# A grouped mixture of experts with its gate, up and down passes in loops of their own

## What is computed

```python
x = layer_norm(ALPHA * x + (1 + g1) * y, ln_mix_g[l], ln_mix_b[l])
h = x * (1 + sc2) + sh2
y = grouped_moe(h, router_w, router_b, w_gate[l], w_up[l], w_down[l])
x = layer_norm(ALPHA * x + (1 + g2) * y, ln_ffn_g[l], ln_ffn_b[l])
...
def expert_block(args):
    xb, e = args
    return (jax.nn.silu(xb @ w_gate[e]) * (xb @ w_up[e])) @ w_down[e]
```

## Time and profile before

| what | us |
| --- | --- |
| median of 3 runs | 1334.7 |
| lowest, highest | 1334.52, 1337.36 |
| the profiled execution as timed | 1341.6 |
| its span, first to last instruction | 1339.5 |
| TensorE busy in it | 1090.9 |
| VectorE busy | 429.8 |
| ScalarE busy | 175.0 |

### The profile page before, as it was taken

How to read it: one execution, slowest core, us unless ns; L and a number is a source line. 1 busy time by engine, 2 the same in 40 slices (tenths; PEclk the granted TensorE clock), 3 DMA queues, 4 the chain that set the end, 5 groups by cost and what they waited for, 6 DMA issues and landing times.

```text
span 1339.5 us, 31050 instructions
## 1 busy us (share of the span) xinstructions
PE 1090.9 (81%) x13118; PEld 644.4 (48%) x13118; DVE 429.8 (32%) x1378; ACT 175.0 (13%) x423; POOL 21.1 (2%) x61
## 2 busy tenths in 40 slices
PE   5999988658998579657899989696599996796675
PEld 1885445224554235323475864363266562463332
DVE  0598152112332113212453431521133331131124
ACT  1104130001010001001201430310011110000011
POOL 1300000000000000000000000000000000000000
PEclk8899989889999889988999999598899998898788
DMA  9975599999999999999996533799999899999990
GB/s 354 383 311 208 224 426 423 425 425 423 424 425 425 425 426 424 424 423 424 416 422 274 239 126 121 321 416 423 425 427 423 342 407 424 425 424 423 424 413 36
DMA packets 56959, 494.74 MB, mean 369 GB/s; under 512 B 4196, under 2 KB 12420, under 8 KB 17176
## 3 DMA queue, kind: packets, MB, share of 16 engines
q1 hardware_dynamic: 55920, 490.75, 88.3%
q10 hardware_dynamic: 744, 2.35, 0.5%
q0 software_dynamic: 192, 0.15, 0.0%
HBM read 492.19 MB, written 1.05 MB: 368 GB/s over the span
## 4 chain that ended last, share of the span: by engine, by line
PE 52%; DMA 41%; DVE 4%; ACT 2%; issue 1%; SPq 0%; DVEq 0%; ACTq 0%; POOLq 0%
PE PS L1122 22%; DMA ring<-in_w_up_dram 17%; DMA ring<-in_w_gate_dram 13%; PE PS L1021 6%; PE PS L1280 4%; DMA ring<-in_w_down_dram 3%; DMA ring<-in_w_kvf_dram 3%; PE PS L1150 2%; DMA work<-in_w_gate_dram 2%; PE PS L1101 2%; PE PS L920 2%; PE PS L1038 2%; DMA ring<-in_w_ada_dram 2%; PE PS L1407 2%; PE PS L1113 1%
## 5 line engine op out<-in xcount | busy, mean ns | idle before, releaser
L1122 PE MATMUL PS<-ring,work 128*32 128x256 f32 x8160 | 518.0, 409 | 171.4 <-DMA ring<-in_w_gate_dram 64.4
L1122 PEld LDWEIGHTS PS<-ring,work 128*32 128x32 f32 x8160 | 280.5, 116 | 391.0 <-issue 116.5
L1728 DVE TENSOR_TENSOR work<-work,PS 128x256 f32<-128x256 f32 x43 | 18.1, 421 | 406.1 <-PE PS L1122 406.1
L1021 PE MATMUL PS<-ring,work 128*128 128x512 f32 x192 | 83.4, 594 | 0.5 <-ACT work L854 0.5
L698 ACT ACTIVATE work<-PS 128x256 f32<-128x256 f32 x43 | 16.5, 384 | 406.0 <-PE PS L1122 406.0
L920 PE MATMUL PS<-ring,cact 128*32 128x512 f32 x384 | 50.7, 668 | 16.1 <-DMA ring<-in_w_ada_dram 16.1
L1101 PE MATMUL PS<-hs,work 128*32 128x256 f32 x784 | 57.7, 414 | 3.8 <-DVE work L1689 3.8
L1280 PE MATMUL PS<-work,ring 128*128 128x256 f32 x256 | 59.0, 394 | 1.4 <-ACT work L630 1.4
L1122 PE MATMUL PS<-work 128*32 128x256 f32 x864 | 52.0, 380 | 9.4 <-DMA work<-in_w_gate_dram 5.4
L1150 PE MATMUL PS<-work 32*128 32x256 f32 x784 | 56.1, 400 | 3.8 <-DVE work L1741 3.8
L1021 PEld LDWEIGHTS PS<-ring,work 128*128 128x128 f32 x192 | 36.2, 190 | 46.5 <-issue 45.7
(11 more groups left out here) (259 smaller groups left out, 871.4 us busy)
## 6 DMA issues: line engine op xcount, KB each, us to landing
ring<-in_w_gate_dram SPq DMA_DIRECT2D x58, 2048.0 KB, 34.3
ring<-in_w_up_dram SPq DMA_DIRECT2D x58, 2048.0 KB, 34.6
ring<-in_w_down_dram SPq DMA_DIRECT2D x58, 2048.0 KB, 28.4
ring<-in_w_ada_dram SPq DMA_DIRECT2D x24, 2048.0 KB, 21.1
work<-in_w_up_dram SPq DMA_DIRECT2D x6, 2048.0 KB, 20.8
work<-in_w_gate_dram SPq DMA_DIRECT2D x6, 2048.0 KB, 33.8
work<-in_w_down_dram SPq DMA_DIRECT2D x6, 2048.0 KB, 42.2
ring<-in_w_pw_dram SPq DMA_DIRECT2D x8, 1024.0 KB, 12.1
```

Source lines behind the costliest of these rows:

```text
L1021: last = pe.matmul(PS[:, banks + 2 * t + q, :], moving[:, k, t * P:(t + 1) * P], quarter(index + h, kk, KH)[:, q * BANK:(q + 1) * BANK], s ...
L1122: last = pe.matmul(dst[SLOTS * s:SLOTS * (s + 1), :], rows[:, cc, SLOTS * q:SLOTS * (q + 1)], quarter(load + h, kk, KH)[:, QUART * s:QUART ...
```

## The change

Four things are changed.

1. All experts but the **first** now run the three loops `gated`, `raised` and `result_of`; only expert 0 keeps `hidden_of`. 
2. In `gated` the next block's token sum stands **ahead** of the gate strips and its transpose between the two strips. VectorE applies the scale into a scratch tile `XM`, waits for `gate_done`, and adds the shift into `XT` (`take_xT_late`).
3. In `raised` VectorE, and no longer ScalarE, copies the kept tokens to `XU`, as the first thing of each block. `XU` is a tile of its own.
4. The final norm is two operations for each token tile: (sum - mean) x gain, then x rstd + offset. ScalarE copies the gain from PSUM to SBUF beforehand (`last_gain`, in `hs`).

ScalarE further waits with its copy to `XT_all` until TensorE has read the residual, which lies in the same memory (`rT_turned`).

```diff
                 def gated(n, j):
                     act.wait_ge(XT_copied, n + l)
+                    act.wait_ge(rT_turned, 2 * l + 2)
                     act.activation(XT_all[:, bass.ds(j * QUART, QUART)], XT.rearrange("p c s -> p (c s)"), ACT.Copy).then_inc(XT_kept, 1)
+                    take_x(n + 1)
                     act.wait_ge(gate_done, n)
                     act.activation(hhT_all[:, bass.ds(j * QUART, QUART)], gate_ps, ACT.Silu).then_inc(sil_ready, 1)
-                    take_x(n + 1)
-
-                def raised(last, j, every):
-                    act.wait_ge(up_done, last)
-                    act.wait_ge(X_turned, every + (l + 1))
-                    act.activation(Xg, XT_all[:, bass.ds(j * QUART, QUART)], ACT.Copy).then_inc(XU_ready, 1)
-                    act.wait_ge(hh_turned, last + 1)
+
+                def raised(n, j):
+                    act.wait_ge(hh_turned, n)
...
             moe(1)
+            act.wait_ge(spread, GAIN_SPREAD)
+            act.activation(last_gain, PS[:, 6:8, :].rearrange("p b n -> p (b n)"), ACT.Copy).then_inc(gain_kept, 1)
...
                     pe.wait_ge(XT_copied, last + (l + 1))
                     pe.wait_ge(hhT_kept, before_all + 1)
                     pe.wait_ge(sil_ready, last)
+                    sum_x(last + 2)
                     strips(load, 0, XT, gate_ps, gate_half)
+                    turn_x(last + 2)
                     strips(load, 1, XT, gate_ps, gate_done)
-                    sum_x(last + 2)
-                    turn_x(last + 2)
...
-                    if e < E - 1:
+                    if e == 0:
                         with pe.Fori(0, blocks):
                             hidden_of(pe.snap(n_pe) + 1, index + 6 * e)
...
+                def take_xT_late(n, kept):
+                    dve.wait_ge(X_turned, n + (l + 1))
...
+                    dve.tensor_tensor(split(XM), split(XT_ps), over[0], ALU.mult).then_inc(XT_begun, 1)
+                    dve.wait_ge(XT_begun, n + (l + 1))
+                    dve.wait_ge(XT_kept, kept)
+                    dve.wait_ge(gate_done, n)
+                    dve.tensor_tensor(XT.rearrange("p c (q s) -> p c q s", q=STRIPS), split(XM), over[1], ALU.add).then_inc(XT_copied, 1)
+
                 def raised(n, j):
+                    dve.tensor_copy(XU, XT_all[:, bass.ds(j * QUART, QUART)]).then_inc(XU_ready, 1)
+                    dve.wait_ge(sil_ready, n)
                     dve.wait_ge(up_done, n)
...
                             next_block(dve.snap(n_dve) + 1)
-                            dve.wait_ge(XT_kept, dve.snap(k_dve) + 1)
-                            take_xT(dve.snap(n_dve) + 2)
+                            take_xT_late(dve.snap(n_dve) + 1, dve.snap(k_dve) + 1)
...
                 for t in range(TT):
+                    link(dve.scalar_tensor_tensor(out=xs[:, t, :].rearrange("p (b n) -> p b n", b=STRIPS),
+                                                  in0=PS[:, 0:STRIPS, QUART * t:QUART * (t + 1)], scalar=mv[:, t, 0:1],
+                                                  in1=last_gain.rearrange("p (b n) -> p b n", b=STRIPS),
+                                                  op0=ALU.subtract, op1=ALU.mult))
+                    dve.scalar_tensor_tensor(out=xs[:, t, :], in0=xs[:, t, :], scalar=rstd[:, t:t + 1], in1=offset,
+                                             op0=ALU.mult, op1=ALU.add).then_inc(done, 1)
```

More of the change, by code:

```diff
@@ L208, in trunk_kernel @@
         r_before = part(E * E, to="p (e f) -> p e f", e=E)
+        XU = r_before.rearrange("p e f -> p (e f)")
         r_hit = part(TT * E, to="p (t e) -> p t e", t=TT)
         r_pos = part(TT * E, to="p (t e) -> p t e", t=TT)
+        XM = work[:, at[0]:at[0] + QUART]
         r_ge = part(2 * GROUPS * PER * PER, to="p (r i j) -> p r i j", i=PER, j=PER)
@@ L276, in trunk_kernel @@
         rT_ready = sem("rT_ready")
+        rT_turned = sem("rT_turned")
         router_in = sem("router_in")
@@ L1076, in residual @@
                                 bank, at = 2 * (k // KH) + half, QUART * t + k % KH
-                                pe.matmul(PS[:, bank, at:at + QUART - 3:KH], rT[of, k, t * P:(t + 1) * P], ident[of, of],
-                                          start=(t == 0 and k % KH == 0), stop=True, tile_position=(64 * half, 0),
-                                          skip_group_check=True)
+                                last = pe.matmul(PS[:, bank, at:at + QUART - 3:KH], rT[of, k, t * P:(t + 1) * P], ident[of, of],
+                                                 start=(t == 0 and k % KH == 0), stop=True, tile_position=(64 * half, 0),
+                                                 skip_group_check=True)
+                                if t == TT - 1 and k == KD - 1:
+                                    last.then_inc(rT_turned, 1)
                 if l == 0:
@@ L1176, in gated @@
                     pe.wait_ge(sil_ready, last)
+                    sum_x(last + 2)
                     strips(load, 0, XT, gate_ps, gate_half)
+                    turn_x(last + 2)
                     strips(load, 1, XT, gate_ps, gate_done)
-                    sum_x(last + 2)
-                    turn_x(last + 2)
                 def raised(n, load, kept, every):
                     pe.wait_ge(XU_ready, kept)
-                    strips(load + 2, 0, XU, up_ps, up_half)
-                    strips(load + 2, 1, XU, up_ps, up_done)
+                    of_kept = XU.rearrange("p (c s) -> p c s", c=NC)
+                    strips(load + 2, 0, of_kept, up_ps, up_half)
+                    strips(load + 2, 1, of_kept, up_ps, up_done)
                     pe.wait_ge(hhT_kept, n)
@@ L1594, in close_sublayer @@
                     return
+                dve.wait_ge(gain_kept, 1)
+                spreads[0] += 1
+                offset = spread_banks(4)
                 for t in range(TT):
-                    last = dve.tensor_scalar(xs[:, t, :].rearrange("p (b n) -> p b n", b=STRIPS),
-                                             PS[:, 0:STRIPS, QUART * t:QUART * (t + 1)], mv[:, t, 0:1], rstd[:, t:t + 1],
-                                             ALU.subtract, ALU.mult)
-                link(last)
-                row = spread_banks(6)
-                for t in range(TT):
-                    last = dve.tensor_tensor(xs[:, t, :], xs[:, t, :], row, ALU.mult)
-                last.then_inc(spread_used, 1)
-                dve.wait_ge(spread_used, spreads[0])
-                with_row(4, lambda t: xs[:, t, :], lambda t: xs[:, t, :], ALU.add, done)
+                    link(dve.scalar_tensor_tensor(out=xs[:, t, :].rearrange("p (b n) -> p b n", b=STRIPS),
[4 more added lines that the diff above has]
+                                             op0=ALU.mult, op1=ALU.add).then_inc(done, 1)
             def ranks(rank, values, rows):
@@ L1718, in next_block @@
                     build_G(n + 1)
+                def take_xT_late(n, kept):
+                    dve.wait_ge(X_turned, n + (l + 1))
+                    split = lambda tile: tile.rearrange("p (c q s) -> p c q s", c=NC, q=STRIPS)
+                    over = [acol[:, (OF_FFN0, OF_FFN1)[l], i, :].rearrange("p (q c) -> p c q", c=NC).unsqueeze(3).to_broadcast([P, NC, STRIPS, SLOTS])
+                            for i in range(2)]
+                    dve.tensor_tensor(split(XM), split(XT_ps), over[0], ALU.mult).then_inc(XT_begun, 1)
[3 more added lines that the diff above has]
+                    dve.tensor_tensor(XT.rearrange("p c (q s) -> p c q s", q=STRIPS), split(XM), over[1], ALU.add).then_inc(XT_copied, 1)
                 def raised(n, j):
+                    dve.tensor_copy(XU, XT_all[:, bass.ds(j * QUART, QUART)]).then_inc(XU_ready, 1)
+                    dve.wait_ge(sil_ready, n)
                     dve.wait_ge(up_done, n)
```

10 lines of the change are left out of this document (6 added, 4 removed).

## The result

The changed kernel takes 1348.3 us (median of 6 runs, 1345.15 to 1352.86) against 1334.6 for the kernel before beside it (6 runs): ratio 1.0102, 95% interval 1.0084 to 1.0121. It is slower by 13.7 us where 6.0 were forecast. The profiled execution took 1346.4 us, its span is 1344.7.

A forecast was written before the change was run, and what follows sets the result against it. Expert stages were taken as DMA-bound, TensorE time counting only where a late load finds the queue empty or behind the last load. +10.7 + 0 - 2.6 - 2.1 = +6.0 gave 1340.7 us; forecast 1337.5 to 1345, range 1331 to 1349.

The forecast's parts named there:

- outer range: Whole kernel: 1331 to 1349 us, taking in no change and most of layer 0's price.
- the lateness in layer 0: Layer 0, blocks 3, 2, 2: -2.7 + 5.9 + 5.9 = 9.1 us late against 11.7 free; cost nought.
- Head wait: Head of each expert: TensorE stands still 2.55 us until VectorE has built the next `G`.
- gate period: Gate loop: 2.00 us wait between blocks plus 4.75 us of work, so one gate block each 6.75 us.
- The up period: Up loop: 1.4 us from up to up with `turn_hh` inside it, so one up pass each 4.85 us.
- The clock rival: Experts 5 and 6: waiting TensorE is granted a lower clock, costing 15 us, time 1356; chance 0.04.
- The stretch: Experts 4, 5, 6 of layer 1: expert 4 ends 2.7 us earlier, expert 6 ends 10.7 us late.
- The 10.1 us to landing: Layer 1, up 0 of expert 8: lands 10.1 us after issue, so cost 10.7 us (8.0 with 7.4 to landing).
- the forecast's own rule: Late loads: lateness costs nothing up to the time to landing less 7.4 us; layer 0 has 11.7 us free.
- Behind the last load: End of kernel: last expert gains 2.6 us (-1.4 gate to up, -1.2 up to up), final norm 2.1.
- Faster: Rival: `G` is ready when asked for, TensorE's stretch gets no longer, DMA hole closes; 1325 us, chance 0.18.
- Slower in both layers: Rival: 0.5 us more on each wait, layer 0 loses 3.9, layer 1 7.5 more; 1352.1 us, chance 0.12.

The follow-up runs named there:

- head_filled: Changed kernel plus 12 matmuls of 128 columns that nobody reads at the head of each expert, ahead of its first token sum: 1.0107 of the kernel before.
- after_again: The changed kernel, unchanged, run and profiled a second time: 1.0096 of the kernel before.
- before_again: The kernel before, unchanged, run and profiled a second time: ratio 0.9992, profiled span 1334.9 us.
- layer0_only: Changed kernel with the new loops of experts 1 to 14 in layer 0 only; last experts and final norm as in the change: 1.0002 of the kernel before.
- last_only_again: Repeat of the changed kernel with the old two loops for all experts but the last: 0.9971 of the kernel before.
- norm_only: Kernel before with only the new final norm (two operations per token tile, ScalarE's copy of the gain): 0.9969 of the kernel before.
- last_only: Changed kernel with the old two loops for all experts but the last, new final norm kept: 0.9959 of the kernel before.
- g_ahead: Changed kernel with VectorE building each block's `G` one block earlier, between the two `XT` operations: 0.9976 of the kernel before.

## Why the prediction was right and wrong

The direction, the mechanism and the place in layer 1 were right, and 1348.3 lies within the outer range of 1331 to 1349, near its end, but over the forecast's own 1337.5 to 1345. The size was not right. The step that failed worst is the lateness in layer 0: it was put at 9.1 us, under the 11.7 that were free, and so its cost at nought, where the lateness was 11.3 to 13.8 and the cost about 3.1. Of the 7.7 us between 6.0 and 13.7, layer 0 makes 3.1, the end 1.3, layer 1 makes 0.9, and 2.4 stay open.

**Each expert's extra time.** Head wait 2.28 (2.55 forecast), between gate blocks 1.62 idle, gate period 6.65 (6.75), copy to `XU` 0.29 (0.30), last up to first down as before: all near. The Trainium skill ("VectorE: DVE Perf Modes", section "Mode 2×_2P — use both read ports for one tensor") gives a float32 copy in SBUF two elements a cycle; L1739 at 0.29 against 0.42 for a tensor-tensor of the same 256 columns agrees in direction. Two things were missing. The up period is 5.15 and not 4.85: the step put `turn_hh` inside the time of VectorE's product and copy, but it can only start behind the product. From the product's end (1061.73) it is 0.15 until it starts, its 0.47 and about 0.20 to the next strip, 0.83 in all, where the forecast had 0.55 for the copy and the signal. And the strip behind a head wait ran mostly at half clock, 3.20 instead of 1.91, which costs 1.2 us an expert by head_filled. The clock rival was given 0.04 and 15 us; it came true in small, with the first strips of experts 5 and 6. Together: 35.1 + 1.2 + 0.3 = 36.6 (37.0 measured) and 52.0 + 1.2 + 0.6 = 53.8 (54.0).

**The stretch.** Expert 4 gained 3.8 us where 2.7 were forecast. So expert 6 is late by -3.8 + 7.9 + 9.5 = 13.6 us (138.2 against 124.6, after_again and before_again), not 10.7.

**From lateness to cost in layer 1.** Up 0 of expert 8 is issued at 1086.7 (1086.2 forecast) and lands at 1095.2 (between 1093.6 and 1096.3). That looks like a hit, and is half one: it was reckoned from a profile of before in which this load landed at 1085.6, while in the repeat it landed at 1082.2. Taken from the first load, the second piece of the table is 415.1 on average in the seven kernels with the old loops in layer 1 and 426.7 in the four with the change's loops: 11.6 us, against 10.7. The 10.1 us to landing, taken as typical of this load, is the upper end: it took 8.4 to 10.1 in the seven kernels with the old loops and 7.7 to 8.5 in the four with the change's. So 2.0 of the 13.6 us of lateness cost nothing.

**Layer 0, forecast at nought.** Its first piece is 498.7 on average in seven kernels with the old loops there and 501.8 in the four with the new: 3.1 us. layer0_only shows the same by time, 1.0002 against 0.9971 on the same chip, 0.31% or 4.1 us. The step that failed is the lateness of 9.1 = -2.7 + 5.9 + 5.9. In layer0_only against last_only_again it is -2.6 + 8.1 + 8.2 = 13.7 by the windows of experts 4, 5 and 6 (46.8, 37.0, 37.2 against 49.4, 28.9, 29.0); there up 0 of expert 8 is issued 13.8 later. The short term is again the expert's own time, 37.0 and 37.2 us where 35.1 were forecast. With the right lateness the forecast's own rule comes out: 13.8 less the 18.6 - 7.7 = 10.9 that were free is 2.9 us, and the load lands 2.9 later. In the two profiles of the change the load is 12.6 and 11.3 late against before and before_again, counted from the landing of gate 0 of expert 0, and lands 1.2 and 2.3 later, where the rule with its 11.7 gives 0.9 and nothing: the direction is the same, and a microsecond or two stays open. That only one of the three late loads was looked at is a second gap. The tightest, down 0 of expert 7, had 6.3 us to spare, but in layer0_only it accounts by itself for 1.2 of the 2.9.

**Behind the last load.** Forecast -2.6 - 2.1 = -4.7. The norm gave -2.4. The last expert gave -2.4 from the landing of its gate 0 on (51.1 to 48.7, norm_only and last_only): 1.5 up to its first up pass (1.4 forecast) and 0.9 from up to up (1.2 forecast); by time that can't be told from nought (0.9965 against 0.9969 for the norm alone). In the change the last piece is 25.1 and 26.2 against 29.6 and 28.4, so -3.4 and not -4.7. What is missing lies in the gate passes of expert 15, for whose head the forecast counted nothing. From the landing of its gate 0 to the end the change takes 50.3 and 51.2 us and not 48.7: in the first TensorE waits 2.49 us for `G` and its first strip takes 3.64, in the second a later strip takes 3.00, behind a wait for data.

**The sum** of the table's pieces is +3.1 + 11.6 - 3.4 = 11.3 us, against 13.7 by the medians. The other 2.4 us stay open. Single executions scatter by about as much or more: the two profiled ones of before took 1341.6 and 1337.0, 7.0 and 2.3 above the median of their runs, those of the change 1.9 below and 0.8 above theirs. The forecast set a difference made on one untypical execution onto the median. That it was untypical stood on record (1341.6 against 1334.7); where its extra time lay, a single profile can't show.

**The rivals.** Faster fell: `G` was not ready, as the listing said, and the kernel that makes it ready (g_ahead) is indeed level with the best, though the 1325 given for it were too low, since its experts of two and three blocks still take 3.2 and 3.8 us longer than before. "Slower in both layers" is what happened, at 1348 and not 1352, and had a chance of 0.12. It should have had more: a margin of 2.6 against 13 waits each unknown to some tenths was no margin. What went beyond the forecast was not in the waits for `G`, which came near it, but in the strips at mostly half clock and the up period.

## What to carry to other kernels

A loop split in two can lay bare dependences that the single loop hid: here four strips of TensorE work stood between a request for `G` and its use, and in the changed kernel none did. Before splitting, or moving a consumer ahead, ask whether its producer can be moved ahead by as much; moving VectorE's `G` up by one block took away 1.2 of the 1.34% that the split cost, by time.

Where weights stream through a ring, ask the margin of **every** load that a late stage releases, and set each against the lateness of what releases it: the margin is issue to landing, less the same for a load into an empty queue. A margin of 2.6 us left over from a sum of many estimated waits is soon used up: in layer0_only two experts took 1.9 and 2.1 us longer than estimated.

## What the hardware did that was not expected

A strip of 32 records takes 1.9 us or up to 3.6 behind waits that look alike. In the changed kernel the head waits of 2.28 and 2.26 us that ended at 999.65 and 1036.62 were followed by slow strips (3.20 and 3.49 us), at a granted clock of 0.57 in 1000 to 1004 and 0.58 in 1037 to 1041, and the one of 2.28 us that ended at 1090.58, at the head of expert 7, by a fast one, at a granted clock of 1.00 in 1091 to 1094:

```profile
1090.58 1.07 PE L1108 MATMUL PS<-hs,work 128*32 128x256 f32 x16 [2.28 <-DVE work L1696]
1091.47 1.91 PE L1129 MATMUL PS<-ring,work 128*32 128x256 f32 x32
```

12 matmuls without use in the gap kept the clock at 1.00 behind the heads of experts 5 and 6 (windows 1001 to 1005 and 1037 to 1041 of head_filled). In expert 4 of that kernel, where none stood in the wait of 2.96 us for data, the clock was 0.66 in 951 to 955. The Trainium skill ("TensorE: Matmul & The Clock Gate", section "Part 1: The HAM clock gate (the "warmup" mystery)") says that the gate looks at how busy TensorE has been recently and that activity releases the throttle. The two slow strips and the filled heads agree. That equal waits differ shows that one wait's length alone doesn't tell; what decides between them, no run here shows.
